# A three-layer float32 kernel, even layer: gate rows spread by transfers, causal mask added on GpSimd

## The reference

```python
log_f = jax.nn.log_sigmoid((fg + b_forget).astype(jnp.float32))   # 512 tokens x 8 heads
c = jnp.cumsum(log_f, axis=1).transpose(0, 2, 1)
...
logits = jnp.einsum('bqhd,bkhd->bhqk', qb, k).astype(jnp.float32) * scale
logits = logits + cq[..., :, None] - c[..., None, :]
logits = jnp.where(mask, logits, NEG_INF)
p = jax.nn.softmax(logits, axis=-1).astype(v.dtype)
```

## Time and profile before

| | |
|---|---|
| median of 3 runs | 2013.41 us (2012.32 to 2014.16) |
| span of the profiled execution | 2010.4 us |
| outside the span, to the median | 3.0 us |
| TensorE busy | 1991.0 us, 99% |
| VectorE busy | 1149.2 us, 57% |
| ScalarE busy | 820.8 us, 41% |
| GpSimd busy | 3.8 us |
| mean granted TensorE clock | 0.998 |

### The profile page before, as it was taken

How to read it: one execution, slowest core, us unless ns; L and a number is a source line. 1 busy time by engine, 2 the same in 40 slices (tenths; PEclk the granted TensorE clock), 3 DMA queues, 4 the chain that set the end, 5 groups by cost and what they waited for, 6 DMA issues and landing times.

```text
span 2010.4 us, 30047 instructions
## 1 busy us (share of the span) xinstructions
PE 1991.0 (99%) x11917; PEld 1608.7 (80%) x11917; DVE 1149.2 (57%) x1896; ACT 820.8 (41%) x1293; POOL 3.8 (0%) x6
## 2 busy tenths in 40 slices
PE   9999999999999999999999999999999999999998
PEld 6776798888888787888888888777777578888888
DVE  6456467534556666567543555877666566424532
ACT  6447544333334454454332333643443432212322
POOL 0000000000000000000000000000000000000000
PEclk9999999999999999999999999999999999999999
DMA  5112122223323211122223224111111122322221
GB/s 192 64 53 84 43 85 92 86 95 105 104 79 110 69 64 64 63 85 86 97 95 102 102 77 142 42 62 33 57 43 44 45 84 103 105 87 102 88 100 63
DMA packets 26992, 165.58 MB, mean 82 GB/s; under 512 B 3200, under 2 KB 3328, under 8 KB 11008
## 3 DMA queue, kind: packets, MB, share of 16 engines
q1 hardware_dynamic: 25872, 161.69, 23.4%
q10 hardware_dynamic: 1008, 2.30, 0.4%
HBM read 160.83 MB, written 2.10 MB: 81 GB/s over the span
## 4 chain that ended last, share of the span: by engine, by line
PE 89%; DVE 6%; ACT 3%; issue 1%; DMA 0%; SPq 0%; DVEq 0%; ACTq 0%
PE bank L474 25%; PE bank L476 24%; PE bank L475 24%; PE bank L1133 2%; PE bank L749 1%; ACT hH L1330 1%; DVE hL L2102 1%; PE bank L957 1%; PE bank L778 1%; PE bank L981 1%; ACT wH L1330 1%; DVE x L2098 1%; PE bank L767 1%; PE bank L1222 1%; PE bank L1220 1%
## 5 line engine op out<-in xcount | busy, mean ns | idle before, releaser
L474 PE MATMUL bank<-hH,wH 128*128 128x512 f32 x1368 | 552.0, 404 | 1.5 <-DVE hL L2064 1.5
L476 PE MATMUL bank<-hH,wL 128*128 128x512 f32 x1368 | 533.7, 390 | 0.0
L475 PE MATMUL bank<-hL,wH 128*128 128x512 f32 x1368 | 533.1, 390 | 0.0
L1330 ACT ACTIVATE wH<-raw 128x2048 fp32r<-128x2048 f32 (+3 forms) x199 | 294.1, 1488 | 116.3 <-PE bank L476 105.1
L474 PEld LDWEIGHTS bank<-hH,wH 128*128 128x128 f32 x1368 | 257.6, 188 | 69.0 <-issue 14.5
L476 PEld LDWEIGHTS bank<-hH,wL 128*128 128x128 f32 x1368 | 257.4, 188 | 54.4
L475 PEld LDWEIGHTS bank<-hL,wH 128*128 128x128 f32 x1368 | 257.9, 189 | 46.1
L2013 DVE TENSOR_TENSOR wL<-raw,wH 128x2048 fp32r<-128x2048 f32 x96 | 219.7, 2289 | 125.6 <-ACT wH L1330 125.6
L474 PE MATMUL bank<-mH,wH 128*128 128x512 f32 (+1 forms) x610 | 233.1, 382 | 0.0
L476 PE MATMUL bank<-mH,wL 128*128 128x512 f32 (+1 forms) x610 | 232.9, 382 | 0.0
L475 PE MATMUL bank<-mL,wH 128*128 128x512 f32 (+1 forms) x610 | 232.9, 382 | 0.0
(11 more groups left out here) (346 smaller groups left out, 2790.5 us busy)
## 6 DMA issues: line engine op xcount, KB each, us to landing
raw<-in_ffn_up SPq DMA_DIRECT2D x44, 1024.0 KB, 4.8
raw<-in_mlp_up SPq DMA_DIRECT2D x16, 1024.0 KB, 4.9
raw<-in_mlp_down SPq DMA_DIRECT2D x16, 1024.0 KB, 4.9
raw<-in_ffn_down SPq DMA_DIRECT2D x16, 768.0 KB, 4.2
raw<-in_odd_in SPq DMA_DIRECT2D x12, 1024.0 KB, 4.8
raw<-in_dn_qkv SPq DMA_DIRECT2D x12, 1024.0 KB, 4.9
raw<-in_ffn_down SPq DMA_DIRECT2D x16, 640.0 KB, 3.8
raw<-in_even_in SPq DMA_DIRECT2D x7, 1024.0 KB, 4.8
```

Source lines behind the costliest of these rows:

```text
L474: mm(out, a, c, start=first, stop=False, skip_group_check=joined)
L475: mm(out, a, d, start=False, stop=False, skip_group_check=joined)
L476: return mm(out, b, c, start=False, stop=last, skip_group_check=joined)
L1330: return nc.scalar.activation(out, in_, func, **kw)
```

## The change

The bias rows go to the 128 partitions by transfers: row h of `gate_rows`, which lies on partition h, is the source 128 times, and `cB` is the destination, 256 KB a head. ScalarE issues those of heads 0 to 3 one after the other as soon as the rows are there, those of heads 4 to 7 at their old slots. The splitting of the rows, the identity and mask in float32r (`constR`), the sixteen spreading matmuls with the eight copies, and the 32 mask matmuls go. GpSimd adds the mask in place to the diagonal block of both heads' bias tiles, once for each of the sixteen query blocks; that of a later block waits until the block before has been biased, as it still needs the block without mask. VectorE waits for it ahead of the bias.

```diff
@@ pair_scores
-                    last = mm(bank[2 + e][:, 0:n], q, k, start=True, stop=g >= 4)
-                    if g >= 4:
-                        last.then_inc(*tick("pair_pe", f"pair.scores{m}.{e}"))
-                if g < 4:
-                    for e in range(2):
-                        mm(bank[2 + e][:, i * P:n], identR, maskR, start=False, stop=True)\
-                            .then_inc(*tick("pair_pe", f"pair.scores{m}.{e}"))
+                    mm(bank[2 + e][:, 0:n], q, k, start=True, stop=True).then_inc(*tick("pair_pe", f"pair.scores{m}.{e}"))
@@ TensorE
-            def gate_spread(h):
...
-                mm(bank[7][:], pick, gate_split[0:H, 0, :], start=True, stop=False)
-                mm(bank[7][:], pick, gate_split[0:H, 1, :], start=False, stop=True).then_inc(*tick("gate_pe", f"gate.spread{h}"))
@@ ScalarE
-            a(identR, ident, ACT.Copy)
-            a(maskR, window[:, FAR:], ACT.Copy)
+            def gate_bias(h):
+
+                if h >= 4:
+                    act.wait_ge(*at(f"pair.biased{4 * (h // 2 - 2) + 3}.1"))
+                act.dma_start(cB[:, h // 2 % 2, h % 2, :], gate_rows[h:h + 1, :].unsqueeze(1).to_broadcast([1, P, SEQ]))\
+                    .then_inc(*tick(f"gate_loaded{h}", f"gate.bias{h}", 16))
...
-            act.wait_ge(*at("gate.negative"))
-            a(gate_split[0:H, 0, :], prob[0:H, 1, 512:1024], ACT.Copy).then_inc(*tick("gate_act", "gate.hi"))
+            act.wait_ge(*at("gate.rows"))
+            for h in range(4):
+                gate_bias(h)
...
-                for h in range(H):
+                for h in range(4, H):
                     if gate_slot(h) == t:
                         gate_bias(h)
@@ VectorE
-                        dve.wait_ge(*at(f"gate.bias{2 * g + e}"))
+                        dve.wait_ge(*at(f"pair.masked{m}"))
...
-            ts(gate_neg, gate_log, -1.0, None, ALU.mult).then_inc(*tick("gate_dve", "gate.negative"))
-            dve.wait_ge(*at("gate.hi"))
-            tt(gate_split[0:H, 1, :], gate_neg, gate_split[0:H, 0, :].bitcast(F32), ALU.subtract).then_inc(*tick("gate_dve", "gate.rows"))
+            ts(gate_rows[0:H, :], gate_log, -1.0, None, ALU.mult).then_inc(*tick("gate_dve", "gate.rows"))
@@ GpSimd
+            def masked(m):
+
+                g, i = m // 4, TT - 1 - m % 4
+                if m % 4:
+                    pool.wait_ge(*at(f"pair.biased{m - 1}.1"))
+                else:
+                    pool.wait_ge(*at(f"gate.bias{2 * g}"))
+                    pool.wait_ge(*at(f"gate.bias{2 * g + 1}"))
+                block_ = cB[:, g % 2, :, i * P:(i + 1) * P]
+                nc.gpsimd.tensor_tensor(block_, block_, window[:, FAR:].unsqueeze(1).to_broadcast([P, 2, P]), ALU.add)\
+                    .then_inc(*tick("pair_pool", f"pair.masked{m}"))
+
+            pool.wait_ge(*at("in.const"))
+            for m in range(16):
+                masked(m)
+            pool.wait_ge(*at("pair.masked15"))
             pool.wait_ge(mm_done, TILE0["even_ukv"] + 1)
             nc.gpsimd.memset(qM[32:64, 1::2, :], 0.0)
```

More of the change, by code:

```diff
@@ L199, in build @@
         xout = sb("xout", [P, TT, DM], F32, base + 4 * 2 * MLP_GROUP * SEQ)
-        cqH, cqL, misc, rope, prob, qF, kF, vF, cB, vM, constR = stage([
+        cqH, cqL, misc, rope, prob, qF, kF, vF, cB, vM = stage([
             ("cqH", [P, 5, SEQ], F32R), ("cqL", [P, 5, SEQ], F32R), ("misc", [P, SEQ]), ("rope", [P, 2, SEQ]), ("prob", [P, 2, 1280]),
-            ("qF", [P, 4, SEQ]), ("kF", [P, 4, SEQ]), ("vF", [P, TT, 512]), ("cB", [P, 2, 2, SEQ]), ("vM", [P, TT, 512]),
-            ("constR", [P, 2, P], F32R)])
-        identR, maskR = constR[:, 0, :], constR[:, 1, :]
+            ("qF", [P, 4, SEQ]), ("kF", [P, 4, SEQ]), ("vF", [P, TT, 512]), ("cB", [P, 2, 2, SEQ]), ("vM", [P, TT, 512])])
         cq_at, qF_at = base + 4 * 5 * SEQ, base + 4 * (13 * SEQ + 2 * 1280)
@@ L207, in build @@
         foxH, foxL = sb("foxH", [P, 4, SEQ], F32R, qF_at), sb("foxL", [P, 4, SEQ], F32R, qF_at + 4 * 4 * SEQ)
-        gate_split = sb("gate_split", [P, 2, SEQ], F32R, qF_at + 4 * 16 * SEQ)
+        gate_rows = sb("gate_rows", [P, SEQ], F32, qF_at + 4 * 16 * SEQ)
         qM, kM = sb("qM", [P, H, SEQ], F32, h_at), sb("kM", [P, H, SEQ], F32, h_at + 4 * H * SEQ)
@@ L780, in pair_values @@
                 last.then_inc(*tick("pair_pe", f"pair.values{g}"))
-            def gate_spread(h):
[L784 to L787, removed]
-                mm(bank[7][:], pick, gate_split[0:H, 0, :], start=True, stop=False)
-                mm(bank[7][:], pick, gate_split[0:H, 1, :], start=False, stop=True).then_inc(*tick("gate_pe", f"gate.spread{h}"))
             def rank_sums():
-                pe.wait_ge(*at(f"gate.bias{H - 1}"))
                 for c, what in enumerate(("cq", "ckv")):
@@ L808, in pair_events @@
                     pair_turn(m)
-                for h in range(H):
-                    if gate_slot(h) == t:
-                        gate_spread(h)
             def first_ready(k):
@@ L1617, in pair_hi @@
                 a(foxH[:, g, :] if g < 4 else hH[:, 2 * g - 8, :], bank[6][:], ACT.Copy).then_inc(*tick("pair_act", f"pair.hi{g}"))
[L1619 to L1624, removed]
             def rank_square(k):
@@ L2347, in _ @@
             even_evict(0)
-            gate_log, gate_z, gate_one, gate_neg = (prob[0:H, e, 512 * c:512 * c + 512] for e in range(2) for c in range(2))
+            gate_log, gate_z, gate_one = (prob[0:H, c // 2, 512 * (c % 2):512 * (c % 2) + 512] for c in range(3))
             dve.wait_ge(evac, 1)
```

## The result

The changed kernel takes **2021.93 us**, median of 4 runs (2021.43 to 2023.80), beside 2013.66 us for the kernel before in runs on the same chip (4 runs, 2012.32 to 2014.16): ratio **1.0043, 95% interval 1.0030 to 1.0056**. That is 8.3 us slower. The spans of the profiled executions differ by 9.8 us (2020.2 for 2010.4).

The account below looks back on a forecast made before the run. TensorE's order of work bounds the kernel. A wait at slot 55 leaves it 13.0 us late with the clock; less 8.3 saved later, plus 0.8 at slot 111, gives +5.5 on 2013.4: 2018.9 us, range 2003 to 2032.

Parts of the forecast that it names:

- the forecast's own case: Transfers above 9.3 and up to 13.3 us make the kernel slower, 2018.9 us forecast; chance 0.38.
- A spread takes 9.9 us, at 26.5 GB/s: Each 256 KB transfer from one partition, rate extrapolated from 128 and 32 source rows, one after the other.
- ScalarE's four issues cost 2.7 us: Issues for heads 0 to 3 at 0.67 us each delay weight unit 3's copies; TensorE waits about 1.0 us at slot 48.
- The granted clock: After TensorE's idle 11 us at slot 55, work runs mostly at 1.2 instead of 2.4 GHz, losing 1.6 us.
- GpSimd's mask, 0.7 us: Each mask addition on GpSimd, 256 columns from two operands, takes 0.7 us ahead of VectorE's bias.
- The rival of GpSimd as the bound: If a mask took 5 us or more, each block would wait for GpSimd; little chance.
- Savings after slot 55, 8.3 us: Six spreads (4.5 us) and masks 2 to 15 (3.8 us) still saved on TensorE after the wait.
- 0.8 us at slot 111: Head 5's row lands at 118.7, so TensorE's transposes at slot 111 wait 0.8 us more.
- Nothing at the MLA heads: GpSimd's two memsets, now after mask 15, end by 173.3, before the scores needing them at 174.72; no cost.
- SyncE's next weight load 2 us later, nothing: SyncE's load goes 2 us later, but its data are used a unit (11 us) later, so it costs nothing.
- The fast rival: Transfers of 1.5 to 5 us hide all but 1.0 us at weight unit 3: 2004.1 us; chance 0.28.
- the slow source row: Sixteen engines at one row, say 20 us a transfer: about 2075 us; chance 0.14 for anything slower than the forecast's own case.

Follow-up runs that it names:

- e7: Kernel before plus six added SBUF-to-SBUF transfers of 2 KB rows (80 or 320 KB each) on SyncE's queue at about 224 us; ran once, 2011.63 us.
- e3: Changed kernel with only heads 0 and 1 issued at once, heads 2 and 3 at slot 57: 2022.06 us, ratio 1.0041 to the kernel before.
- e10: Kernel before plus six added 256 KB transfers from SBUF rows to 128 partitions on SyncE's queue at about 224 us; ran once, 2035.00 us.
- e6: Changed kernel with gate rows stored to HBM and spread from there, two heads a transfer: 2005.49 us, ratio 0.9957 to the kernel before.

## Why the prediction was right, and where it was not

The side and the size were right (2018.9 predicted, 2021.9 measured), but the measured loss is 8.3 us where 5.5 were forecast (9.8 between the two profiles), and its mechanism differs in one step of weight. The range of 2003 to 2032 held both sides, and the forecast's own case had a chance of 0.38, so part of the hit is luck.

- *A spread takes 9.9 us, at 26.5 GB/s*: measured 27 GB/s. The second row was expected at 60.7 and block 0's mask began at 61.06; the fourth at 80.5 and that mask began at 80.18. The slope through two rates that differ by a factor of four in source rows gave the right number for 1 row out of 128, by luck: by the same slope four neighbouring rows would be about twice as fast as one, and e7 shows them no faster. What counts is how many groups of partitions are read, not how many rows. The Trainium skill's page "SBUF — State Buffer", section "Door 1: The DMA port swizzle", puts the limit at a group of partitions, and the measurement of e7 agrees: 0 to 3 take 5.00 us, one of them alone 4.65, four apart 2.49. Its 27.6 GB/s for one group is close to the 27 measured here, where a single source is read 128 times.
- *ScalarE's four issues cost 2.7 us*: **the step that failed.** They cost 17.6 (0.58 + 0.62 + 6.77 + 9.61). The price came from kM's issues, which were only two, and fast ones. Nothing bounded it from above by what the third and fourth issue cost while the first two are under way. So TensorE's wait came at slot 48, 16.5 us long, instead of 1.0 us there and 11 us at slot 55. Block 2's scores were 16.6 us late for 12.7 expected, and e3, which takes the third and fourth issue away, brings 12.25. That is the 4 us between forecast and measurement. It is less than the 15 us that the blocking lasts, since the bias rows would have held TensorE for most of them anyway.
- *The granted clock*: 1.6 us of loss expected behind the wait. The step matmuls of 256 columns come every 0.21 us from 62.7 to 64.9, then every 0.12; from the scores of block 0 to those of block 1 it took 8.22 us (60.67 to 68.89) where 6.50 less the mask pair, 6.23, had been enough (45.55 to 52.05): 2.0 us lost. The size was about right, the place is another slot.
- *GpSimd's mask, 0.7 us*: 0.72 to 0.74 in ten of the sixteen, 1.12 to 1.72 in the others. VectorE waited for it once, 3.7 us ahead of block 8; what came late there was head 5's row, for which GpSimd itself had waited until 120.32, and TensorE worked on. The rival of GpSimd as the bound was rightly given little.
- *Savings after slot 55, 8.3 us*: from block 2 (+16.6) to block 15 (+8.5) 8.1 us were worked off.
- *0.8 us at slot 111*: not there. The row of head 5 landed at about 120.2 and the scores start at 124.13 without a wait, since the kernel was 3 us later than forecast.
- *Nothing at the MLA heads*: TensorE waits 1.18 us for the transfers `qM<-sq`. The prediction asked only whether GpSimd's later memsets end before the scores; it put at nothing what they do to VectorE, whose two divisions beside them took 2.89 us instead of 0.62 and made the rotated queries late. It costs 0.8 us from block 15 (+8.5) to the MLA head (+9.3).
- *SyncE's next weight load 2 us later, nothing*: it was issued at 60.64 instead of 42.98, and beside the spreads its 1 MB took 19.8 us to land instead of 4.8. TensorE did not have to wait for it.
- *The fast rival* (one partition delivers what 32 did) is out by the rate; *the slow source row* (20 us a transfer) as well.

## What to carry to other kernels

A broadcast inside SBUF from one partition runs at one group's 27 GB/s, however wide it writes: send a row through HBM and read it from there, or spread the sources four partitions apart within one transfer (the second way was measured only by itself, in e7 and e10). Do not price a row of issues by its first two: where transfers are slow, the third can hold the engine that issues it, with everything that stands behind it in its order; slow transfers belong on a queue whose engine has nothing urgent next. When work moves to GpSimd, look at which VectorE instructions it will run beside. And before judging a part that is worth 2 or 3 us, look at whether the stretch it saves in and the total agree.

## What had not been expected

- ScalarE's queue took two transfers of 256 KB at 27 GB/s in 0.6 us each; the third issue blocked for 6.77 us, the fourth for 9.61, about the time of one transfer. They were through at 47.4 and 57.1 us, 3.9 and 3.8 us before the first and the second transfer landed. That a full queue is the reason is read from these times; how much it holds was not measured.
- A slow transfer on ScalarE's queue slows a weight load on SyncE's: 1 MB landed after 4.8 us before, 19.8 after and 16.8 in e3; in e6, behind the two reads from HBM on its own queue, after 8.3.
- Two VectorE divisions of 128x256 took 0.62 us before and 2.89 beside GpSimd's memsets.
- 256 KB to 128 partitions: 11.20 us from one partition, 6.68 from two, 4.57 from four and 3.11 from sixteen, four apart. A store of 16 KB to HBM and two reads of 512 KB, each row read 128 times, were done from 38.51 to about 47 us; with the weight load beside them the engines moved up to 389 GB/s.
- Writing has the limit too: 80 KB to partitions 64 to 67 took 4.68 us, to four partitions four apart 2.49.
- Two transfers on two queues from two groups hardly overlapped (landings 11.2 and 18.8 us after the issues, from one group 11.8 and 21.0); open why.
